# Expert stage of a hybrid mixer/PEER step: V rows gathered per token instead of per slot, weighted sum as a contraction over 128 experts

## The reference, cut to what matters

```python
PK_HEADS, N_KEYS, PK_TOPK = 8, 128, 16            # 16384 experts, width 1024
def _peer(h, p):
    qh = (ht @ p['pk_w_q']).reshape(t, PK_HEADS, 2, PK_DH)
    s = jnp.einsum('thpd,phkd->pthk', qh, p['pk_sub_keys'])
    sv, si = lax.top_k(s, PK_TOPK)
    cand = sv[0][..., :, None] + sv[1][..., None, :]
    best, pos = lax.top_k(cand.reshape(t, PK_HEADS, 256), PK_TOPK)
    eidx = ...                                     # expert number of each place
    gate = jax.nn.softmax(best, axis=-1)
    # per block of 128 tokens: hb (128, 1024), eb and gb (128, 8, 16)
    act = jax.nn.gelu(jnp.einsum('td,thkd->thk', hb, u_tab[eb]))
    return jnp.einsum('thk,thkd->td', gb * act, v_tab[eb])
```

## Time and profile before

| what | value |
|---|---|
| median of 3 runs | 4477.78 us |
| the 3 runs | 4476.44 to 4484.85 us |
| span of the profiled execution, first to last instruction | 4473.8 us |
| PE busy | 3754.3 us (84%) |
| DVE busy | 2602.6 us (58%) |
| POOL busy | 1282.6 us (29%) |
| ACT busy | 1077.7 us (24%) |
| mean over the span of what the DMA engines moved | 293 GB/s |

### The profile page before, as it was taken

How to read it: one execution, slowest core, us unless ns; L and a number is a source line. 1 busy time by engine, 2 the same in 40 slices (tenths; PEclk the granted TensorE clock), 3 DMA queues, 4 the chain that set the end, 5 groups by cost and what they waited for, 6 DMA issues and landing times.

```text
span 4473.8 us, 40368 instructions
## 1 busy us (share of the span) xinstructions
PE 3754.3 (84%) x10642; PEld 1830.8 (41%) x10642; DVE 2602.6 (58%) x6424; ACT 1077.7 (24%) x2678; POOL 1282.6 (29%) x1174
## 2 busy tenths in 40 slices
PE   8999999999967788877878887787888887887777
PEld 3766766555433333333333333333333333333222
DVE  4544545233257676666566656666666666666555
ACT  3444543000012222222222222212222222222211
POOL 0000000000014334444343434443443343334433
PEclk9999999999989999999999999999999999999999
DMA  4000002211559999999999998999999999999998
GB/s 167 21 27 28 17 8 89 97 66 52 193 213 355 388 354 400 368 395 370 391 374 379 397 387 362 394 398 366 382 394 378 376 393 394 382 367 398 421 422 360
DMA packets 187700, 1310.84 MB, mean 293 GB/s; under 512 B 24082, under 2 KB 25618, under 8 KB 36274
## 3 DMA queue, kind: packets, MB, share of 16 engines
q0 software_dynamic: 165888, 1208.03, 66.9%
q1 hardware_dynamic: 21684, 101.33, 5.9%
HBM read 1299.28 MB, written 10.00 MB: 293 GB/s over the span
## 4 chain that ended last, share of the span: by engine, by line
PE 56%; DMA 23%; issue 9%; DVE 7%; ACT 3%; POOL 1%; DVEq 0%; POOLq 0%; SPq 0%; ACTq 0%
PE ps L530 23%; DMA arena<-in_uv,arena 22%; PE ps L1097 8%; PE ps L449 8%; PE ps L490 5%; PE ps L473 3%; DVE arena L843 2%; ACT arena L625 2%; PE ps L1141 1%; PE ps L1091 1%; PE ps L1158 1%; POOL arena L415 1%; DVE arena L779 1%; DVE arena L715 1%; PE ps L504 1%
## 5 line engine op out<-in xcount | busy, mean ns | idle before, releaser
L530 PE MATMUL ps<-arena 128*128 128x512 f32 x4608 | 2226.2, 633 | 618.0 <-ACT arena L625 617.6
L843 DVE CUSTOM_DVE_ANT_0 arena<-arena 128x1024 f32<-128x1024 f32 x1152 | 1407.9, 1224 | 767.2 <-DMA arena<-in_uv,arena 703.6
L415 POOL DMA_INDIRECT arena<-in_uv,arena x1152 | 1276.4, 1108 | 1919.9 <-PE ps L530 1760.0
L530 PEld LDWEIGHTS ps<-arena 128*128 128x128 f32 x4608 | 888.1, 200 | 1907.7 <-ACT arena L625 953.2
L625 ACT ACTIVATE arena<-ident,arena 128x128 f32<-128x128 f32 x1152 | 398.3, 393 | 1200.9 <-DVE arena L832 1200.8
L1097 PE MATMUL ps<-arena 128*128 128x384 f32 x1152 | 388.5, 494 | 15.1 <-issue 13.2
L449 PE MATMUL ps<-arena 128*128 128x384 f32 x1152 | 373.7, 487 | 2.5 <-DMA arena<-in_w_mg 2.5
L406 POOL IOTA arena<- 128x16 f32 x1 | 0.1, 145 | 1244.6 <-DMA x_scratch<-arena 1244.6
L1097 PEld LDWEIGHTS ps<-arena 128*128 128x128 f32 x1152 | 218.0, 193 | 160.3 <-issue 23.0
L449 PEld LDWEIGHTS ps<-arena 128*128 128x128 f32 x1152 | 218.2, 190 | 159.7 <-issue 6.0
L619 ACT ACTIVATE arena<-arena 128x2 f32<-128x2 f32 x576 | 116.2, 202 | 663.2 <-DVE arena L843 662.7
(11 more groups left out here) (200 smaller groups left out, 2463.8 us busy)
## 6 DMA issues: line engine op xcount, KB each, us to landing
arena<-in_w_mod SPq DMA_DIRECT2D x12, 2048.0 KB, 23.3
arena<-in_uv,arena POOLq DMA_INDIRECT x1152, 9.9
arena<-in_w_in SPq DMA_DIRECT2D x28, 512.0 KB, 3.3
arena<-in_w_mg SPq DMA_DIRECT2D x8, 1536.0 KB, 6.5
arena<-x_scratch SPq DMA_DIRECT2D x18, 512.0 KB, 11.9
arena<-in_w_q SPq DMA_DIRECT2D x4, 2048.0 KB, 20.9
arena<-in_xT SPq DMA_DIRECT2D x4, 1152.0 KB, 13.4
arena<-in_x_tok SPq DMA_DIRECT2D x9, 512.0 KB, 4.6
```

Source lines behind the costliest of these rows:

```text
L415: nc.gpsimd.indirect_dma_start(out=RG[:, s, :], out_offset=None, in_=uv, in_offset=bass.IndirectOffsetOnAxis(ap=IDXS[:, par_, s:s + 1], ax ...
L530: mm = nc.tensor.matmul(PS[:, n, :], DG[:, s, :], RG[:, s, D + n * 512:D + (n + 1) * 512], start=False, stop=False, skip_group_check=True)
L843: ins = v.tensor_tensor_reduce(RG[:, s, 0:D], RG[:, s, 0:D], H2C, 1.0, 0.0, ALU.mult, ALU.add, PRE[:, s:s + 1])
```

## The change

The gather is split in two. U rows are still gathered per slot, with the token on the partition (`fetch_u`, 0.5 MB each, eight buffers `UR`), and DVE's dot of a slot frees its buffer. V rows are gathered per token: the 128 experts of one token go to the 128 partitions (`fetch_v`, 0.5 MB, eight buffers `VR`). For that the expert numbers of a tile are transposed by PE (`indices_turned`), and so are the coefficients (`coefs_turned`), once per tile. ACT copies a coefficient column of each token into a block of 32 columns `CX` that is zero otherwise (`columns`, four times a tile), and PE contracts over the 128 experts: tokens c x 32 + g, c = 0 to 3, form group g; each has its own column group of 32 of the PE array and adds into its own 32 partitions of the sum (`values`).

The coefficients of a tile exist only when all its dots are done, so the V work of a tile runs one phase after its U work: ten phases for nine tiles. In phase p POOL issues the U gather of slot k of tile p and the V gather of the k-th token of tile p - 1 in turn. All loops of the stage are unrolled, and the places of the routing steps are given anew.

```diff
+    UR = AR[:, A_RING:A_RING + RING * D].rearrange("p (s c) -> p s c", s=RING)
+    VR = AR[:, A_RING + RING * D:A_B].rearrange("p (s c) -> p s c", s=RING)
+    uv_rows = uv.rearrange("e (h d) -> (e h) d", h=2)
+    FRONT_AT, PAIR_AT, TOP_AT = 1, (2, 9, 16, 23), 16
...
     def stage_b_pool(pool):
-        def fetch(r, par_, first=False):
-            pool.wait_ge(idx_r, r + 1)
-            for s in range(RING):
-                if not first:
-                    wait_alone(pool, v_used, r * RING + (s + 1 - RING))
-                nc.gpsimd.indirect_dma_start(
-                    out=RG[:, s, :], out_offset=None, in_=uv,
-                    in_offset=bass.IndirectOffsetOnAxis(ap=IDXS[:, par_, s:s + 1], axis=0),
-                ).then_inc(gathered[s], 16)
+        def fetch_u(t, s):
+            n = t * SLOTS + s
+            if s % (2 * TOPK) == 0:
+                pool.wait_ge(pair_done, t * PAIRS + s // (2 * TOPK) + 1)
+            if n >= RING:
+                wait_alone(pool, dots, n + 1 - RING)
+            nc.gpsimd.indirect_dma_start(out=UR[:, s % RING, :], ..., in_=uv_rows,
+                in_offset=bass.IndirectOffsetOnAxis(ap=EIDX[t % 2][:, s:s + 1], axis=0),
+            ).then_inc(u_in[s % RING], 16)
+        def fetch_v(t, k):
+            n = t * SLOTS + k
+            if k == 0:
+                pool.wait_ge(eft_e, t + 1)
+            if n >= RING:
+                wait_alone(pool, v_used, n + 1 - RING)
+            j = token_of(k)
+            ...
+        for p in range(TILES + 1):
+            for k in range(SLOTS):
+                if p < TILES:
+                    fetch_u(p, k)
+                if p > 0:
+                    fetch_v(p - 1, k)
...
     def stage_b_pe(pe):
+        def values(t, g):
+            if g == 0:
+                pe.wait_ge(acc_free, t)
+            if g % PIECE == 0:
+                pe.wait_ge(cx_r, t * (QUAD // PIECE) + g // PIECE + 1)
+            for half in range(2):
+                for c in range(4):
+                    k = 4 * g + c
+                    if half == 0:
+                        pe.wait_ge(v_in[k % RING], 16 * ((t * SLOTS + k) // RING + 1))
+                    mm = nc.tensor.matmul(PS[c * QUAD:(c + 1) * QUAD, half, :], CX[:, c, g % PIECE, :],
+                                          VR[:, k % RING, half * 512:(half + 1) * 512],
+                                          start=(g == 0), stop=(g == GROUPS - 1))
+                    if half == 1:
+                        mm.then_inc(v_used, 1)
...
     def stage_b_act(act):
-                    for s in range(g * GRP, (g + 1) * GRP):
-                        A(DG[:, s, :], ident[:], ACT.Copy, scale=COEF[:, s:s + 1]).then_inc(diag_r, 1)
+        def gelu_of(t):
+            act.wait_ge(dots, (t + 1) * SLOTS)
+            A(GEL, PRE[t % 2], ACT.Gelu_apprx_tanh).then_inc(gel_r, 1)
...
     def stage_b_dve(dve):
+        def dot(t, s):
+            dve.wait_ge(u_in[s % RING], 16 * ((t * SLOTS + s) // RING + 1))
+            v.tensor_tensor_reduce(UR[:, s % RING, :], UR[:, s % RING, :], H2[t % 2], 1.0, 0.0, ALU.mult,
+                                   ALU.add, PRE[t % 2][:, s:s + 1]).then_inc(dots, 1)
...
+        for p in range(1, TILES + 1):
+            ...
+            for s in range(SLOTS):
+                if p < TILES:
+                    dot(p, s)
+                if s == 0:
+                    ...                       # end.read_sum(), indices(p)
+                elif s == 1:
+                    coef(p - 1)
+                ...                           # front at s = 3, residual at 7, norm at 10
+                if p + 1 < TILES and s >= TOP_AT:
+                    r, n = s - TOP_AT, SLOTS - TOP_AT
+                    for step in steps[r * len(steps) // n:(r + 1) * len(steps) // n]:
+                        step()
```

More of the change, by code:

```diff
@@ L298, in build @@
     BEST, POS = sm(2, TOPK), sm(2, TOPK, dt=U32)
-    PRE, GEL, COEF = sm(RING), sm(RING), sm(RING)
+    PRE = [sb(f"dots{n}", [P, P])[:] for n in range(2)]
+    extra = AR[:, A_B + 16 * D:A_END]
+    EIDXT = [extra[:, n * P:(n + 1) * P].bitcast(U32) for n in range(2)]
+    EF = extra[:, 2 * P:3 * P]
+    GEL, COEF, CT = ones[:], mask_f[:], mask_b[:]
     PHL = sb("places", [P, 2, 2, TOPK], U32)[:]
@@ L523, in rounds @@
-        def rounds(t, i, between):
-            for q in range(RPP):
-                for s in range(RING):
-                    n0 = (t * ROUNDS + i * RPP + q) * RING + s + 1
-                    pe.wait_ge(diag_r, n0)
-                    for n in range(2):
-                        mm = nc.tensor.matmul(PS[:, n, :], DG[:, s, :], RG[:, s, D + n * 512:D + (n + 1) * 512],
-                                              start=False, stop=False, skip_group_check=True)
-                    mm.then_inc(v_used, 1)
-                    at = (q * RING + s + 1) / GRP - 1
-                    if at in between:
-                        between[at]()
@@ L537, in clear, with front_step @@
-        def clear():
-            for n in range(2):
-                nc.tensor.matmul(PS[:, n, :], zero[:], zero[:, 0:1].to_broadcast([P, 512]),
-                                 start=True, stop=False, skip_group_check=True)
-        def tile(t, last=False):
-            pe.wait_ge(acc_free, t)
-            clear()
-            rounds(t, 0, {} if last else {1: lambda: front(t + 1)} | pair_between(t + 1, 0))
-            with pe.Fori(1, PAIRS) as i:
-                rounds(t, i, {} if last else pair_between(t + 1, i))
+        def front_step(tn, g):
+            if g == FRONT_AT:
+                front(tn)
+            for i in range(PAIRS):
+                b = PAIR_AT[i]
+                if g == b:
+                    queries(tn, i, range(4))
+                elif g == b + 1:
+                    queries(tn, i, range(4, KD))
+                    turn(tn, i)
+                elif g == b + 2:
+                    score(tn, i)
@@ L550, in stage_b_pe @@
         front(0)
-        for i in range(2):
+        for i in range(PAIRS):
             pair(0, i)
         pe.wait_ge(mix_f, TILES)
-        clear()
-        rounds(0, 0, two_pairs_between(0, 2))
-        rounds(0, 1, {1: lambda: front(1)} | pair_between(1, 0))
-        rounds(0, 2, pair_between(1, 1))
-        rounds(0, 3, two_pairs_between(1, 2))
-        with pe.Fori(1, TILES - 1) as t:
-            tile(t)
-        tile(TILES - 1, last=True)
+        indices_turned(0)
+        front(1)
+        for i in range(PAIRS):
+            pair(1, i)
@@ L564, in stage_b_act @@
+        for p in range(1, TILES + 1):
+            if p < TILES:
+                indices_turned(p)
+            coefs_turned(p - 1)
+            for g in range(GROUPS):
+                values(p - 1, g)
+                if p + 1 < TILES:
+                    front_step(p + 1, g)
     def stage_b_act(act):
@@ L629, in end, with front_step @@
             A(st[:, 3:4], st[:, 2:3], ACT.Sqrt, bias=eps[:], scale=1.0 / D).then_inc(e_sd, 1)
-        def front_between(tn):
-            return {0: lambda: row_norm(tn), 2: lambda: rows_out(tn)} | pair_between(tn, 0)
-        def tile(t, last=False):
-            rounds(t, 0, {3: lambda: end(t - 1)} | ({} if last else front_between(t + 1)))
-            with act.Fori(1, PAIRS) as i:
-                rounds(t, i, {} if last else pair_between(t + 1, i))
+        def front_step(tn, g):
+            if g == FRONT_AT - 1:
+                row_norm(tn)
+            if g == FRONT_AT:
+                rows_out(tn)
+            for i in range(PAIRS):
+                b = PAIR_AT[i]
+                if g == b + 1:
+                    queries_out(tn, i)
+                    turned_out(tn, i)
+                elif g == b + 2:
+                    scores_out(tn, i)
+                elif g == min(b + 7, GROUPS - 1):
+                    gates(tn, i)
         row_norm(0)
         rows_out(0)
-        for i in range(2):
+        for i in range(PAIRS):
             queries_out(0, i)
@@ L645, in stage_b_act @@
             gates(0, i)
-        rounds(0, 0, two_pairs_between(0, 2))
-        rounds(0, 1, front_between(1))
-        rounds(0, 2, pair_between(1, 1))
-        rounds(0, 3, two_pairs_between(1, 2))
-        with act.Fori(1, TILES - 1) as t:
-            tile(t)
-        tile(TILES - 1, last=True)
+        row_norm(1)
+        rows_out(1)
+        for i in range(PAIRS):
+            queries_out(1, i)
+            turned_out(1, i)
+            scores_out(1, i)
+            gates(1, i)
+        for p in range(1, TILES + 1):
+            gelu_of(p - 1)
+            coef_out(p - 1)
+            for g in range(GROUPS):
+                if g % PIECE == 0:
+                    columns(p - 1, g // PIECE)
+                if g == 2 and p >= 2:
+                    end(p - 2)
+                if p + 1 < TILES:
+                    front_step(p + 1, g)
         end(TILES - 1)
@@ L958, in stage_b_dve @@
         end.norm()
-    c_shift = sem("shifted")
     block = ctx.enter_context(nc.Block())
```

279 lines of the change are left out of this document (123 added, 156 removed).

## The result

The changed kernel takes **4667.88 us** (median of 4 runs, 4649.32 to 4681.04) against 4478.21 us for the kernel before: a ratio of 1.0418, 95% interval 1.0392 to 1.0444. Timed again later, it took 4670.03 us against 4480.66 (ratio 1.0439, 1.0408 to 1.0469). The forecast was 4562 us, slower by 1.9%. The direction and the range held, but the loss is more than twice the forecast's.

What follows compares the result with a forecast made beforehand. DMA engines were taken as nearly the bound, with POOL the pace-setter after the change. Span 1542 + 2816 + 5 + 179 + 16 = 4558 us, plus 4 gives 4562 us, 1.9% slower; range 4408 to 4715.

Steps and rivals of the forecast that it cites:

- T: Phases 1 to 8, one U plus one V gather: 2.75 us, ends 2.56 and 2.90, from gathers phased against dots.
- rival 2: Gathers beside dots: locks at random or worse, T 2.87 to 3.0, time 4685 to 4818 us; chance 0.11.
- About a fifth of the slots run faster, while DVE waits for scores: Full phases: these slots run at the DMA's 2.56 us a pair while DVE waits for late scores.
- POOL: Gather issue: near 2304 x 1.08 us busy, 2480 us and more, idle before a gather mostly "issue", DMA share some 0.93.
- DMA at no more than 410 GB/s for 4 KB rows: Gathers of 4 KB packets: at most 410 GB/s against 422 with 8 KB, so 1.28 us a gather.
- PE hides, columns side by side: Value matmuls: four side by side at best, at worst 7.1 us for four tokens against 11 available; hidden either way.
- Rival 3: Value matmuls: columns not side by side and PE at 1.2 GHz, 14 us over 11 available; 4600 to 4690 us, chance 0.12.
- ACT's diagonals and the shorter chain free 34 us a tile, then POOL is next: Buffer release: 1152 diagonals and the long dot-to-matmul chain go, removing 34 us a tile; POOL is late next.
- Phase 0: First phase, U gathers alone: DVE-bound, gathers start at 1276.5 us, first gather of phase 1 at 1542.
- Phase 9: Last phase, 128 V gathers alone: pitch 1.40 us from the ring of eight, 179 us, ends 164 and 220.
- Break-even at T = 2.67: Whole kernel: equal time to the kernel before at 2.67 us a pair; each 0.01 us of T moves 10 us.
- Rival 1: Full phases: DMA sets the pace, T 2.56 to 2.66, time 4367 to 4470 us; chance 0.31.

Runs made afterwards that it cites:

- e3: Changed kernel with PE's query and score steps one to three groups earlier and DVE's searches from slot 24 instead of 16; 4645.55 us, ratio 1.0377.
- e14: Changed kernel with every matmul of the weighted sum issued twice, that part of the output doubled, second measurement; 4705.7 us, ratio 1.0503.
- e2: Changed kernel with the dot reading h from PSUM, copied there once a tile, and scores and turned coefficients moved to other banks; 4443.9 us, ratio 0.9921.
- e11: Changed kernel with h in PSUM and, in the last phase, V gathers also using the eight U buffers, second measurement; 4416.94 us, ratio 0.9858.

## Why the prediction was right in direction and wrong in size

By its own terms, span against span (4558 forecast, 4667.5 measured, 109.5 us too little):

- **T, the pair of gathers: the step that failed.** Forecast 2.75 us, measured 2.87 over phases 1 to 7. 7 x 128 x 0.12 = 107 us, nearly all of the miss. In phase 8 it was 2.61, which gave back 18. Over all eight phases it was 2.84, inside the ends that I gave (2.56 and 2.90): the lock as the cost was right, its size was not.
- The argument behind 2.75 had two faults, which pull in opposite directions. First, it took 4.4 us from a U gather's start to its dot, from gathers after a pause (one of them had paused 3.82 us, not "5 us or more"). With the queues full it is longer: in the timeline of the changed kernel the median is 6.6 us in phase 3 and 7.9 in phase 8. The fixed phase worked out from 4.4 was therefore not the one that sets in; the one of phase 8 costs the lock 15 us in all (about 1.02 us for V, 0.94 for U), and T is less than 2.75 there. Second, there is no fixed phase beside routing, and this made the miss. What happens there is close in cost to "locks at random", rival 2 with its chance of 0.11, but not the same mix: the forecast's working for it gave 2.90 us (38% of gathers inside a dot, 0.55 lost each), the count gives 48% and 0.39 each, 2.87. The starts are not spread evenly: 249 of the 868 fall into the first 0.3 us of a dot and lose 208 us together, 378 come more than 0.9 us into it and lose 18. The time that rival 2 named, 4685 and more, was not reached, because phase 8 ran at 2.61. Beside routing, then, the upper end of my T was near the right value. The last tile of the old kernel, from which I took comfort, had no routing; the stretch with routing gave 1116 ns, so 2.83, and was the nearer row.
- *"About a fifth of the slots run faster, while DVE waits for scores":* the opposite. What DVE leaves undone it then does back to back, and its dots at 1.15 us hold gather after gather (the rows at 3455 to 3463 us). e3 prices it at some 22 us, hardly more than the noise. As for the waits themselves, I had put them at some 400 us; they were 236, and cost nothing directly, as said.
- *POOL:* right. Over 2480 us busy (2561.6), idle mostly "issue", DMA share 0.97 rather than 0.93.
- *DMA at no more than 410 GB/s for 4 KB rows:* right, 405 GB/s in phase 8.
- *PE hides, columns side by side:* right (e14, and the starts in phase 9). Its busy time in the value matmuls did not halve (1759.5 us against 2226.2 before); those groups hold modelled ends, and the granted clock was lower. Rival 3 fell.
- *ACT's diagonals and the shorter chain free 34 us a tile, then POOL is next:* right in kind. What the change would have brought without the lock is e2's phases of 331 to 337 us against 353, so 16 to 22 of the 34 us; some 9 of the rest are the slower 4 KB rows (2.56 against 2.49 us a pair). What the diagonals and the chain are each worth was not run.
- *Phase 0:* gathers of U alone from 1278.7, 271.6 us, against 266 from 1276.5, so it ends 8 us after the forecast.
- *Phase 9:* 195 us from first to last gather against 179, and 17 to the end against 16 and 5 for the handover: 12 us more in all. The pitch of 1.52 was set by the ring of eight, as argued; with 16 buffers it is 1.29 (e11).
- *Break-even at T = 2.67:* consistent. e2 runs at 331 to 337 us a phase, T = 2.6, and is faster.

Rival 1 (the DMA sets the pace) was the right picture for e2, not for this change.

## What to carry to other kernels

When a change makes an engine the pace-setter, price its instruction as it runs beside the others, not bare. A lock worth 14 us behind slack was worth 225 without it. Before halving a transfer to gain freedom, count the instructions that issue it, and if DVE must read two tensors meanwhile, put the one that stays (here h) in PSUM. And where two programs that should be alike differ, run the same one in another session before explaining it.

## What the runs showed of the hardware that I had not expected

- One PSUM operand in place of an SBUF operand in the dot took the mean gather from 1.09 to 1.13 us down to 0.95 and left the dot at 1.22 us: 225 us of 4668 for one operand.
- The lock is one-sided here: a gather waits for a dot (it ends 0.81 us after the dot does), and none of the 817 dots that start inside a gather is longer for it.
- Dots back to back and gathers fall into step so that one can hold a gather after another: 1.97, 1.94, 1.99 and 1.86 us beside 0.94.
- A program took 4749 to 4764 us in the 5 runs of one session and 4416 to 4419 in the 8 of two others, of which one was on the same chip. The cause is open.
